# Adding up gathered expert rows on the tensor engine: a diagonal of slot weights as stationary operand instead of a scaled row and eight transposing matmuls

## The chip, the cores and the metric

One Trainium2 chip, one of its cores. The metric is the device time of one execution in microseconds (us), the median over the runs shown. The engines are named as in the profile: PE (TensorE; PEld are its weight loads), DVE (VectorE), ACT (ScalarE), POOL (GpSimd) and SP (SyncE, which only issues transfers here).

## The reference

One decoder layer over 1024 positions of width 1024, all in float32: an S5 group and an attention group side by side, an output projection, and then a PEER layer, which is where the change lies. For each position the PEER layer takes 8 heads, finds for each the 16 best of 128 x 128 experts, and adds up 128 expert rows:

```python
idx = e1 * PEER_N_KEYS + e2
g = jax.nn.softmax(top_s, axis=-1).astype(hc.dtype)
u = expert_down[idx]
a = jax.nn.gelu(jnp.einsum('thkd,td->thk', u, hc))
return jnp.einsum('thk,thkd->td', g * a, expert_up[idx])
...
return x + gate_f * peer_ffn(h2, w_query, sub_keys, expert_down, expert_up)
```

The host lays `expert_down` and `expert_up` beside each other, so that one gathered row of 2048 values holds both.

## The kernel before, in words

Three short phases come first (modulation and input projection, the S5 recurrence, the latent projections of the attention). The last phase, `phase_ef`, takes some 85% of the time. It is one loop over 1024 **slots**, written out in the same order on every engine. The 1024 positions are 8 tiles of 128 (one position per partition); slot n belongs to tile n // 128 and is one (head, rank) pair of it. For slot n:

- POOL (L1192) gathers 128 rows of 8 KB, one per partition, with an indirect DMA into `pair[n % 9]`: columns 0 to 1023 are the down row, 1024 to 2047 the up row. Before it may, it waits until `up_used` has reached n - 8, that is until PE has finished with the buffer's last content.
- DVE (L1693, `dot`) multiplies the down row by `h2` and sums it into one value per position, `a`.
- ACT (`gelu`) takes the GELU of that value (L1488), multiplies it by the gate `g` into `w` (L1490), and scales the 1024 columns of the up row by `w` in place (L1492), which counts `scaled` up.
- PE (`add_up`, L1357) waits for `scaled` and runs eight transposing matmuls of 128 x 128 against the identity. They add into one of two PSUM accumulators, `acc_a` and `acc_b`, so that a tile's sum over its 128 slots stands there transposed (model column on the partition).

After a tile's last slot, DVE's `finish` (L1700) multiplies the sum by the gate column `mod` into `gated`, PE's `turn_back` (L1366) transposes it back in eight steps into the PSUM tile `turns`, and DVE's `close` (L1706) adds the residual `x2s` and leaves the result in `h2`, from where SP stores it.

Into this loop other work is set at fixed slots by tables of the kernel (`AT_SCORES`, `AT_TURN`, `AT_VALUES`, `AT_EXP`, `PROJECT`, `ASKED`, `SCORED`, `WEIGHED`): the attention of tiles 2 to 7 at slots 8 to 188; the output projection of those tiles at slots 191 to 246 (24 pieces of 4 matmuls of 512 columns); the query projections for later slots (`queries`, L1332, 16 matmuls of 128 columns, about one group for every 16 slots) with their scores (L1342); and the exponentials of the gates (`softened`, L1483, for every second group of 16 slots), for which ACT loads another table and, for the next GELU, loads that one again. Every engine works its list strictly in order.

Of the kernel before, what the change touches and what calls it, by code (L numbers as in the profile page):

```python
# [16 lines left out]
ALU = mybir.AluOpType  # L17
ACT = mybir.ActivationFunctionType
AX = mybir.AxisListType

P = 128
D = 1024
KD = D // P
SEQ = 1024
NT = SEQ // P
# [12 lines left out]
PH, PK, TOPK = 8, 128, 16  # L38
# [14 lines left out]
SHIFT_M, SCALE_M, GATE_M, SHIFT_F, SCALE_F, GATE_F = 0, 8, 16, 24, 32, 40  # L53
# [31 lines left out]
def place(nc, name, shape, kb, dt=FP32):  # L85
    return nc.alloc_sbuf_tensor_at(name, shape, dt, offset=BIG + int(kb * KB))
# [6 lines left out]
def bcast(ap, axis, shape):  # L93
    return ap.unsqueeze(axis).to_broadcast(shape)
# [844 lines left out]
def phase_ef(nc, A, S):  # L939
# [22 lines left out]
    qt_pair = place(nc, "qt_pair", [P, 2, 2, P], 149)  # L962
    pieces = place(nc, "pieces", [P, 2, KD, PK], 152)
    x2s = place(nc, "x2s", [P, D], 152)
    gated = place(nc, "gated", [P, KD, P], 156)
    h2t = place(nc, "h2t", [P, 2, KD, P], 160)
    staged = place(nc, "staged", [P, 10, 2, PK], 168)
    cand = place(nc, "cand", [P, TOPK, TOPK], 178)
# [2 lines left out]
    sk = place(nc, "sk", [P, 2, PK], 180)  # L971
    qt_one = place(nc, "qt_one", [P, 2, P], 182)
    wq = [place(nc, f"wq{n}", [P, 4, KD, PK], kb) for n, kb in enumerate((136, 32, 48, 64))]
    row_cols = (S.mod[:, GATE_M:GATE_M + KD], S.a_f[:], S.mod[:, SHIFT_F:SHIFT_F + KD])
    yst_kept = nc.dram_tensor("yst_kept", (P, NT - FIRST, KS, P), FP32, kind="Internal").ap()
    rows_kept = nc.dram_tensor("rows_kept", (P, 3, D), FP32, kind="Internal").ap()

# [55 lines left out]

    ACC = (0, 0, 0, 1, 0, 1, 0, 1)
    END = {P * (i + 1) + (1 if i < 2 else 8): i for i in range(NT - 1)}

    with ExitStack() as ctx:
        small = lambda *a: ctx.enter_context(nc.sbuf_tensor(*a))
# [32 lines left out]
        piece_in = [sem(f"g_piece{n}") for n in range(2)]  # L1071
        wq_in = [sem(f"g_wq{n}") for n in range(4)]
        pair_in = [sem(f"g_pair{n}") for n in range(R)]
        dotted, up_used, w_ready, ga_ready, scaled = sem("g_dot"), sem("g_upused"), sem("g_w"), sem("g_ga"), sem("g_sc")
        less_ready, exp_ready, idx_ready, g_ready = sem("g_less"), sem("g_exp"), sem("g_idx"), sem("g_gate")
        t_done, q_done, q_out, s_done, s_out, s_read = (sem(f"g_{n}") for n in ("t", "q", "qo", "s", "so", "sr"))
        acc_read, fin_ready, stored, spilled, x2s_in, back_done = (sem(f"g_{n}") for n in ("acc", "fin", "st", "spill", "x2s", "back"))
        block = ctx.enter_context(nc.Block())
        tile = lambda i: slice(i * P, (i + 1) * P)
        half = lambda buf, m: buf[:, (m % 2) * 512:(m % 2) * 512 + 512] if items[m][0] < 4 else buf[:]  # L1080
# [114 lines left out]
        @block.tensor  # L1195
        def _(pe):
            t = nc.tensor
            evicted = {"act": 0, "dve": 0, "closed": 0}
            waited = dict(evicted)
            turned_out, yat_out, pts_out = {}, {}, {}  # L1200

            def turns_free():
                for name, s in (("act", tt_out), ("dve", b_read), ("closed", fin_ready)):
                    if evicted[name] > waited[name]:
                        pe.wait_ge(s, evicted[name])
                        waited[name] = evicted[name]
# [138 lines left out]
            def add_up(n):  # L1345
                i = n // P
                if n == 0:
                    pe.wait_ge(a_out, FIRST)
                elif n % P == 0 and i < 3:
                    pe.wait_ge(acc_read, i)  # L1350
                elif n == 3 * P:
                    pe.wait_ge(a_out, NT)
                elif n % P == 0:
                    pe.wait_ge(acc_read, i - 1)
                pe.wait_ge(scaled, n + 1)
                for k in range(KD):
                    last = t.matmul(accs[ACC[i]][:, k * P:(k + 1) * P], pair[n % R][:, D + k * P:D + (k + 1) * P], S.ident[:],  # L1357
                                    is_transpose=True, start=n % P == 0 and k % 4 == 0, stop=n % P == P - 1,
                                    skip_group_check=True)
                last.then_inc(up_used, 1)  # L1360

            def turn_back(i):
                pe.wait_ge(acc_read, i + 1)
                turns_free()
                for k in range(KD):
                    last = t.transpose(tt[:, k * P:(k + 1) * P], gated[:, k, :], S.ident[:])  # L1366
                last.then_inc(back_done, 1)
                evicted["closed"] = i + 1

            row(0)  # L1370
            at_scores(0)
# [25 lines left out]
            for n in range(SLOTS):  # L1397
                if n in AT_SCORES:
                    at_scores(AT_SCORES[n])
                if n in AT_BACK:  # L1400
                    at_back(AT_BACK[n])
                if n in AT_TURN:
                    at_turn(AT_TURN[n])
                if n in AT_VALUES:
                    at_values(AT_VALUES[n])
                for part_ in range(2):
                    if n - part_ in PROJECT:
                        project_ssm(PROJECT[n - part_], (part_,))
                    if n - 4 - part_ in PROJECT:
                        project_att(PROJECT[n - 4 - part_], (part_,))  # L1410
                if n in TURNED:
                    turn(TURNED[n])
                if n in ASKED:
                    queries(ASKED[n], (0,) if WIDE(ASKED[n]) else (0, 1))
                if n - 2 in ASKED and WIDE(ASKED[n - 2]):
                    queries(ASKED[n - 2], (1,))
                if n in SCORED:
                    scores(SCORED[n])
                if n - 2 in END:
                    turn_back(END[n - 2])  # L1420
                add_up(n)
            turn_back(NT - 1)

        @block.scalar
        def _(act):
# [59 lines left out]
            def gelu(n):  # L1485
                k = (n // TOPK) % (2 * PH)
                act.wait_ge(dotted, n + 1)
                s_.activation(ga[:, n % NA:n % NA + 1], a[:, n % NA:n % NA + 1], ACT.Gelu_apprx_tanh).then_inc(ga_ready, 1)  # L1488
                act.wait_ge(ga_ready, n + 1)
                s_.activation(w[:, n % NA:n % NA + 1], ga[:, n % NA:n % NA + 1], ACT.Copy, scale=g[:, k, n % TOPK:n % TOPK + 1]).then_inc(w_ready, 1)  # L1490
                act.wait_ge(w_ready, n + 1)
                s_.activation(pair[n % R][:, D:], pair[n % R][:, D:], ACT.Copy, scale=w[:, n % NA:n % NA + 1]).then_inc(scaled, 1)  # L1492

            for m in range(EARLY):
                at_exp(m)
# [46 lines left out]
        def _(dve):  # L1542
# [139 lines left out]
            def weigh(batch):  # L1682
                first, end = BATCHES[batch]
                at_, to = first % (2 * PH), (end - 1) % (2 * PH) + 1
                dve.wait_ge(exp_ready, batch + 1)
                own.step(v.tensor_reduce(gs[:, at_:to], g[:, at_:to, :], AX.X, ALU.add))
                own.step(v.reciprocal(gs[:, at_:to], gs[:, at_:to]))
                v.tensor_tensor(g[:, at_:to, :], g[:, at_:to, :], bcast(gs[:, at_:to], 2, [P, end - first, TOPK]), ALU.mult).then_inc(g_ready, 1)

            def dot(n):  # L1690
# [2 lines left out]
                v.scalar_tensor_tensor(down, down, 1.0, h2[:, n // P, :], ALU.mult, ALU.mult,  # L1693
                                       accum_out=a[:, n % NA:n % NA + 1]).then_inc(dotted, 1)

            def finish(i):
                dve.wait_ge(up_used, P * (i + 1))
                if i == 0:
                    dve.wait_ge(q_done, PH + 1)
                v.tensor_tensor(gated[:], accs[ACC[i]][:].rearrange("p (k n) -> p k n", n=P),  # L1700
                                bcast(S.mod[:, GATE_F:GATE_F + KD], 2, [P, KD, P]), ALU.mult).then_inc(acc_read, 1)

            def close(i):
                dve.wait_ge(back_done, i + 1)
                dve.wait_ge(x2s_in, 16 * (i + 1))
                v.tensor_tensor(h2[:, i, :], tt[:], x2s[:], ALU.add).then_inc(fin_ready, 1)  # L1706

            at_top(0)
            for m in range(EARLY):
# [24 lines left out]
            for n in range(SLOTS):  # L1734
                dot(n)
                if n in FOUND:
                    find_part(*FOUND[n])
                if n in AT_TOP:
                    at_top(AT_TOP[n])
                if n - 1 in AT_BACK:  # L1740
                    at_back(AT_BACK[n - 1])
                if n in AT_TURNED:
                    at_turned(AT_TURNED[n])
                if n in AT_NORMAL:
                    at_normal(AT_NORMAL[n])
                if n - 8 in PROJECT:
                    combine(PROJECT[n - 8])
                if n - 9 in PROJECT:
                    add_x(PROJECT[n - 9])
                if n - 13 in PROJECT:  # L1750
                    make_h2(PROJECT[n - 13])
                if n - 14 in PROJECT:
                    shift_h2(PROJECT[n - 14])
                if n in WEIGHED:
                    own.wait()
                    weigh_less(WEIGHED[n])
                if n - 2 in WEIGHED:
                    weigh(WEIGHED[n - 2])
                if n in END:
                    finish(END[n])  # L1760
                if n - 3 in END:
                    close(END[n - 3])
# [49 lines left out]
```

## Time and profile before

| | |
|---|---|
| runs | 3248.62, 3248.66, 3250.68 us; median 3248.66 |
| span of the profiled execution | 3247.0 us |
| PE busy | 2362.8 us (73%) |
| DVE busy | 2206.0 us (68%) |
| ACT busy | 2035.2 us (63%) |
| POOL busy | 1321.2 us (41%) |
| gathered by the indirect DMA | 1077.61 MB, its packets 81% of 16 engines' span |
| L1357 (the additions) on PE | 8192 matmuls, 878.7 and 592.6 us in the two accumulators |
| L1492 (the scaling) on ACT | 1024 times 1149 ns |

The profiled execution's own time is its span, 3247.0 us, 1.7 us under the median of the runs. "Busy" is the union of an engine's instructions. The granted clock is the share of TensorE's 2.4 GHz that it was given; at any moment it is 1.0 (2.4 GHz) or 0.5 (1.2 GHz), and the numbers between are means over a stretch. A float32 matmul that multiplies stands in the trace as two MATMUL records and two LDWEIGHTS records; a transposing one as one of each.

### The profile page before, as it was taken

What the parts mean: (1) busy time and instruction counts of PE and PEld (TensorE: products, weight loads), DVE (VectorE), ACT (ScalarE), POOL (GpSimd) and SP (SyncE); (2) the same over time, 40 slices, a digit from 0 to 9 for tenths busy, and PEclk for the clock granted to TensorE, in tenths of its full rate; (3) what the DMA queues carried; (4) which work ended last, traced back from release to release, by engine and by line L of the source; (5) the groups of instructions that cost most, each with busy time, mean ns of one, the idle gap of its engine ahead of it and who ended that gap; (6) DMA issues with size and microseconds to landing.
All of it is one profiled execution on the core that took longest, in us unless ns stands there. A gap on an engine that the chain in (4) does not pass through costs nothing.

```text
span 3247.0 us, 38518 instructions
## 1 busy us (share of the span) xinstructions
PE 2362.8 (73%) x13186; PEld 1943.1 (60%) x13186; DVE 2206.0 (68%) x5266; ACT 2035.2 (63%) x3762; POOL 1321.2 (41%) x1190
## 2 busy tenths in 40 slices
PE   5977787777778797676676677766767667776766
PEld 4654456666666565565665566665666566665655
DVE  6881547767778576677666666666666666666654
ACT  3313416767777566676666766676667766766665
POOL 1140313323434344444445454444444444544543
PEclk9988998988878798777767776777677777767766
DMA  6600039988888999999999999999999999999997
GB/s 250 189 14 4 34 146 419 386 320 322 345 335 346 418 419 420 420 421 421 421 422 420 418 421 419 419 411 420 421 419 413 419 417 418 415 417 419 418 420 326
DMA packets 175461, 1162.57 MB, mean 358 GB/s; under 512 B 22720, under 2 KB 23632, under 8 KB 43808
## 3 DMA queue, kind: packets, MB, share of 16 engines
q0 software_dynamic: 148352, 1077.61, 81.0%
q1 hardware_dynamic: 25680, 78.30, 6.5%
q10 hardware_dynamic: 1232, 4.20, 0.3%
q8 instruction: 104, 1.70, 0.2%
q14 instruction: 93, 0.76, 0.1%
HBM read 1147.32 MB, written 11.53 MB: 357 GB/s over the span
## 4 chain that ended last, share of the span: by engine, by line
DMA 33%; DVE 23%; PE 16%; ACT 11%; issue 4%; POOL 1%; POOLq 0%; DVEq 0%; SPq 0%
DMA pair<-in_experts_dram,idx_g 32%; DVE pair L1693 11%; PE acc_a L1357 5%; ACT pair L1492 5%; PE pef L1332 3%; PE acc_b L1357 2%; ACT L1488 2%; PE acc_b L1237 1%; ACT w L1490 1%; PE pef L1256 1%; ACT pex L1433 1%; DVE top_i L1621 1%; DVE staged L1622 1%; ACT ga L1488 1%; DVE top_i L1624 1%
## 5 line engine op out<-in xcount | busy, mean ns | idle before, releaser
L1192 POOL DMA_INDIRECT pair<-in_experts_dram,idx_g x1024 | 1215.8, 1187 | 1484.1 <-PE acc_a L1357 865.1
L1693 DVE SCALAR_TENSOR_TENSOR pair<-pair,h 128x1024 f32<-128x1024 f32 x1024 | 1247.3, 1221 | 666.2 <-DMA pair<-in_experts_dram,idx_g 664.7
L1357 PE MATMUL acc_a<-ident,pair 128*128 128x128 f32 x5120 | 878.7, 333 | 443.2 <-ACT pair L1492 435.4
L1492 ACT ACTIVATE pair<-pair,w 128x1024 f32<-128x1024 f32 x1024 | 1176.2, 1149 | 33.3
L1357 PEld LDWEIGHTS acc_a<-ident,pair 128*128 128x128 f32 x5120 | 738.1, 173 | 576.3 <-ACT pair L1492 546.0
L1357 PE MATMUL acc_b<-ident,pair 128*128 128x128 f32 x3072 | 592.6, 361 | 292.9 <-ACT pair L1492 292.4
L1357 PEld LDWEIGHTS acc_b<-ident,pair 128*128 128x128 f32 x3072 | 488.6, 187 | 391.4 <-ACT pair L1492 386.7
L1488 ACT ACTIVATE ga<-a 128x1 f32<-128x1 f32 x1024 | 204.1, 199 | 687.3 <-DVE pair L1693 682.5
L1490 ACT ACTIVATE w<-ga,g 128x1 f32<-128x1 f32 x1024 | 301.6, 295 | 33.2
L1332 PE MATMUL pef<-h2t,wq 128*128 128x128 f32 x1536 | 196.6, 291 | 1.6 <-DMA wq<-in_w_query_t_dram 1.6
L1332 PEld LDWEIGHTS pef<-h2t,wq 128*128 128x128 f32 x1536 | 195.0, 209 | 2.8 <-issue 2.8
L1563 DVE TENSOR_SCALAR_CACHE_REDUCE pex<-acc_b 128x128 f32<-128x128 f32 (+7 forms) x64 | 48.3, 754 | 83.1 <-PE turns L1245 43.8
L1237 PE MATMUL acc_b<-kt,qt 96*128 96x512 f32 (+3 forms) x192 | 95.2, 582 | 0.3 <-DVE pex L1563 0.2
L1256 PEld LDWEIGHTS pef<-v,pts 128*128 128x128 f32 x576 | 78.8, 212 | 10.3 <-issue 4.8
L1693 DVE DVE_READ_ACCUMULATOR pair<-pair,h 128x1 f32 x1024 | 84.5, 82 | 0.0
L1256 PE MATMUL pef<-v,pts 128*128 128x64 f32 x576 | 80.3, 290 | 3.6 <-DVE pts L1574 2.1
L401 DVE SCALAR_TENSOR_TENSOR wada<-wada,silu_c 128x1024 f32<-128x1024 f32 x48 | 57.5, 1221 | 18.3 <-DMA wada<-in_w_ada_t_dram 17.7
L1332 PE MATMUL pef<-h2t,pieces 128*128 128x256 f32 (+1 forms) x288 | 64.0, 383 | 3.5 <-ACT h2t L1459 2.2
L1488 ACT ACT_TABLE_LOAD x50 | 64.2, 1283 | 0.9
L1574 DVE COPY pts<-turns 128x128 f32<-128x128 f32 (+7 forms) x64 | 48.2, 753 | 21.5 <-PE pef L1256 14.0
L1467 ACT ACTIVATE qt_one<-pef 128x256 f32<-128x256 f32 x50 | 19.1, 382 | 69.0 <-PE pef L1332 68.9
L1332 PEld LDWEIGHTS pef<-h2t,pieces 128*128 128x128 f32 x288 | 54.6, 214 | 12.1 <-issue 3.4
(341 smaller groups left out, 2365.6 us busy)
## 6 DMA issues: line engine op xcount, KB each, us to landing
wada<-in_w_ada_t_dram SPq DMA_DIRECT2D x48, 512.0 KB, 5.8
pair<-in_experts_dram,idx_g POOLq DMA_INDIRECT x1024, 16.2
pieces<-in_w_query_t_dram SPq DMA_DIRECT2D x16, 512.0 KB, 8.2
wq<-in_w_query_t_dram SPq DMA_DIRECT2D x4, 2048.0 KB, 35.9
ht<-in_x_t_dram ACTq DMA_DIRECT2D x4, 1024.0 KB, 15.1
wout_a<-in_w_out_dram SPq DMA_DIRECT2D x1, 4096.0 KB, 13.1
x2s<-out_dram SPq DMA_DIRECT2D x8, 512.0 KB, 12.3
out_dram<-h SPq DMA_DIRECT2D x8, 512.0 KB, 8.9
```

The lines of the kernel that those rows point to most:

```text
L401: v.scalar_tensor_tensor(wb, wb, 1.0, silu_c[:], ALU.mult, ALU.mult, accum_out=macc[:, b:b + 1]).then_inc(w_used, 1)
L1192: p.indirect_dma_start(pair[n % R], None, A["experts"], bass.IndirectOffsetOnAxis(ap=idx[:, t % (2 * PH), k:k + 1], axis=0)).then_inc(pair ...
L1237: last = t.matmul(sc[:, b:end], S.qt[:, i, h, :], S.kt[:, h, b:end], start=not diagonal, stop=True, skip_group_check=True)
L1256: last = t.matmul(ob[:, h * DV:(h + 1) * DV], half(pts, m)[:, b * P:(b + 1) * P], S.v[:, b, h * DV:(h + 1) * DV], start=b == 0, stop=b == i)
L1332: last = t.matmul(view(qs[:, n * wide:(n + 1) * wide]), weight[:, k, :], h2t[:, :, k, :] if WIDE(q) else h2t[:, min(to, 1), k, :], start=k ...
L1357: last = t.matmul(accs[ACC[i]][:, k * P:(k + 1) * P], pair[n % R][:, D + k * P:D + (k + 1) * P], S.ident[:], is_transpose=True, start=n % ...
L1488: s_.activation(ga[:, n % NA:n % NA + 1], a[:, n % NA:n % NA + 1], ACT.Gelu_apprx_tanh).then_inc(ga_ready, 1)
L1490: s_.activation(w[:, n % NA:n % NA + 1], ga[:, n % NA:n % NA + 1], ACT.Copy, scale=g[:, k, n % TOPK:n % TOPK + 1]).then_inc(w_ready, 1)
L1492: s_.activation(pair[n % R][:, D:], pair[n % R][:, D:], ACT.Copy, scale=w[:, n % NA:n % NA + 1]).then_inc(scaled, 1)
L1563: v.tensor_scalar(probs(m)[:, 0:n], half(pb, m)[:, 0:n], -SCALE, None, ALU.mult, ALU.min, accum_out=top[:, m:m + 1]).then_inc(top_ready, 1)
L1574: v.tensor_copy(half(pts, m)[:, 0:n], half(tt, m)[:, 0:n]).then_inc(tt_out, 1)
L1693: v.scalar_tensor_tensor(down, down, 1.0, h2[:, n // P, :], ALU.mult, ALU.mult, accum_out=a[:, n % NA:n % NA + 1]).then_inc(dotted, 1)
```

## The change

ACT no longer scales the up row. It writes a 128 x 128 diagonal instead, the identity with each row scaled by that position's `w`, into the single tile `diag`. PE takes `diag` as stationary operand and passes the up row, as it was gathered, through it as moving operand: two float32 matmuls of 512 columns. The sum then stands in PSUM with the position on the partition. The eight transposes back at a tile's end go away; for them a row of the gate, `grow`, is made once at slot 126 (`gate_row` on PE, `gate_row_out` on DVE), and `finish` and `close` work on 1024 columns as before.

```diff
-    gated = place(nc, "gated", [P, KD, P], 156)
+    grow = place(nc, "grow", [P, D], 156)
+    diag = place(nc, "diag", [P, P], 199)
...
-                pe.wait_ge(scaled, n + 1)
-                for k in range(KD):
-                    last = t.matmul(accs[ACC[i]][:, k * P:(k + 1) * P], pair[n % R][:, D + k * P:D + (k + 1) * P], S.ident[:],
-                                    is_transpose=True, start=n % P == 0 and k % 4 == 0, stop=n % P == P - 1,
-                                    skip_group_check=True)
+                pe.wait_ge(diag_ready, n + 1)
+                for m in range(2):
+                    last = t.matmul(accs[ACC[i]][:, m * 512:(m + 1) * 512], diag[:], pair[n % R][:, D + m * 512:D + (m + 1) * 512],
+                                    start=n % P == 0, stop=n % P == P - 1, skip_group_check=True)
                 last.then_inc(up_used, 1)
 
-            def turn_back(i):
-                pe.wait_ge(acc_read, i + 1)
+            def gate_row():
                 turns_free()
                 for k in range(KD):
-                    last = t.transpose(tt[:, k * P:(k + 1) * P], gated[:, k, :], S.ident[:])
-                last.then_inc(back_done, 1)
-                evicted["closed"] = i + 1
+                    last = t.transpose(tt[:, k * P:(k + 1) * P], row_cols[3][:, k:k + 1].to_broadcast([P, P]), S.ident[:])
+                last.then_inc(rows_done, 1)
+                evicted["gate_row"] = 4
...
-                s_.activation(pair[n % R][:, D:], pair[n % R][:, D:], ACT.Copy, scale=w[:, n % NA:n % NA + 1]).then_inc(scaled, 1)
+                if n >= 1:
+                    act.wait_ge(up_used, n)
+                s_.activation(diag[:], S.ident[:], ACT.Copy, scale=w[:, n % NA:n % NA + 1]).then_inc(diag_ready, 1)
...
+            def gate_row_out():
+                dve.wait_ge(rows_done, 4)
+                dve.wait_ge(q_done, PH + 1)
+                v.tensor_copy(grow[:], tt[:]).then_inc(rows_out, 1)
...
-                v.tensor_tensor(gated[:], accs[ACC[i]][:].rearrange("p (k n) -> p k n", n=P),
-                                bcast(S.mod[:, GATE_F:GATE_F + KD], 2, [P, KD, P]), ALU.mult).then_inc(acc_read, 1)
+                v.tensor_tensor(h2[:, i, :], accs[ACC[i]][:], grow[:], ALU.mult).then_inc(acc_read, 1)
...
-                v.tensor_tensor(h2[:, i, :], tt[:], x2s[:], ALU.add).then_inc(fin_ready, 1)
+                v.tensor_tensor(h2[:, i, :], h2[:, i, :], x2s[:], ALU.add).then_inc(fin_ready, 1)
```

PE's list before, at a query group in the later part of the loop (`g_sc` is the semaphore `scaled`; L1357 is `add_up`, L1332 `queries`):

```order
L1357 MATMUL acc_b<-ident,pair8_2704 128x128 [waits g_sc]
L1357 MATMUL acc_b<-ident,pair8_2704 128x128 x7
L1332 MATMUL pef1<-h2t_2716,wq2_2725 128x128 [waits g_wq2,g_so,e_tto]
L1332 MATMUL pef1<-h2t_2716,wq2_2725 128x128 x7
L1332 MATMUL pef1<-h2t_2716,wq2_2725 128x128 [waits g_wq2]
L1332 MATMUL pef1<-h2t_2716,wq2_2725 128x128 x7
L1357 MATMUL acc_b<-ident,pair0_2696 128x128 [waits g_sc]
L1357 MATMUL acc_b<-ident,pair0_2696 128x128 x7
```

The same place of PE's list in the changed kernel (`g_dg` is `diag_ready`; L1359 is `add_up`, L1334 `queries`):

```order
L1359 MATMUL acc_b<-pair8_2704,diag_2716 128x512
L1334 MATMUL pef1<-h2t_2717,wq2_2726 128x128 [waits g_wq2,g_so,e_tto]
L1334 MATMUL pef1<-h2t_2717,wq2_2726 128x128 x7
L1334 MATMUL pef1<-h2t_2717,wq2_2726 128x128 [waits g_wq2]
L1334 MATMUL pef1<-h2t_2717,wq2_2726 128x128 x7
L1359 MATMUL acc_b<-pair0_2696,diag_2716 128x512 [waits g_dg]
L1359 MATMUL acc_b<-pair0_2696,diag_2716 128x512
L1359 MATMUL acc_b<-pair1_2697,diag_2716 128x512 [waits g_dg]
```

No work is moved here: the queries stand between the same slots, and each slot's eight matmuls have become two.

ACT's list before, around the exponentials of the gates (L1488 is the GELU, L1490 `w`, L1492 the scaling, L1483 the exponential):

```order
L1490 ACTIVATE w<-ga,g 128x1 [waits g_ga]
L1492 ACTIVATE pair3_2699<-pair3_2699,w 128x1024 [waits g_w]
L1483 ACT_TABLE_LOAD
L1483 ACTIVATE g<-g 128x32 [waits g_less]
L1488 ACT_TABLE_LOAD
L1488 ACTIVATE ga<-a 128x1 [waits g_dot]
L1490 ACTIVATE w<-ga,g 128x1 [waits g_ga]
L1492 ACTIVATE pair4_2700<-pair4_2700,w 128x1024 [waits g_w]
```

The same place of ACT's list in the changed kernel (L1487 the GELU, L1489 `w`, L1493 the diagonal; `g_upused` is `up_used`):

```order
L1489 ACTIVATE w<-ga,g 128x1 [waits g_ga]
L1493 ACTIVATE diag_2716<-ident,w 128x128 [waits g_upused,g_w]
L1482 ACT_TABLE_LOAD
L1482 ACTIVATE g<-g 128x32 [waits g_less]
L1487 ACT_TABLE_LOAD
L1487 ACTIVATE ga<-a 128x1 [waits g_dot]
L1489 ACTIVATE w<-ga,g 128x1 [waits g_ga]
L1493 ACTIVATE diag_2716<-ident,w 128x128 [waits g_upused,g_w]
```

The order is the same; what ACT writes is one tile for all slots instead of nine buffers in turn, and each write now waits for PE as well.

## Rows read from the trace of the kernel before

**Rows 1.** The page: span, clock and DMA share in 40 slices, issues (median to landing).

```profile
span 3247.0 us, 38518 instructions
...
PEclk9988998988878798777767776777677777767766
DMA  6600039988888999999999999999999999999997
...
pair<-in_experts_dram,idx_g POOLq DMA_INDIRECT x1024, 16.2
```

**Rows 2.** L1492 alone, once per slot, in three stretches: duration min/median/max, first and last start.

```profile
L1492 ACT ACTIVATE pair<-pair,w x192: 1147/1148/1160, 493.1 to 1089.6; 128x1024 f32<-128x1024 f32 x192
...
L1492 ACT ACTIVATE pair<-pair,w x759: 1147/1148/1155, 1312.8 to 3237.2; 128x1024 f32<-128x1024 f32 x190
```

**Rows 3.** Windows: length, busy PE, PEld, DVE, ACT, POOL; clock, DMA share, GB/s.

```profile
493.00:1093.00 600.00, 459.10 (x2848) 394.69 (x2848) 444.36 (x1113) 427.24 (x764) 225.58 (x203) 0.84 0.91 357
1093.00:1313.00 220.00, 180.32 (x908) 124.75 (x908) 145.82 (x265) 135.86 (x249) 92.70 (x86) 0.89 1.01 419
1313.00:3240.00 1927.00, 1349.89 (x7772) 1160.28 (x7772) 1324.41 (x3217) 1332.55 (x2439) 904.58 (x751) 0.72 1.01 416
```

**Rows 4.** Timeline near the end: start, duration, engine, what [idle before, releaser].

```profile
3226.07 1.97 PE L1357 MATMUL acc_b<-ident,pair 128*128 128x128 f32 x8 [0.79 <-ACT pair L1492]
...
3226.80 0.20 ACT L1488 ACTIVATE ga<-a 128x1 f32<-128x1 f32 x1 [0.78 <-DVE pair L1693]
3227.04 0.30 ACT L1490 ACTIVATE w<-ga,g 128x1 f32<-128x1 f32 x1
...
3229.27 0.20 ACT L1488 ACTIVATE ga<-a 128x1 f32<-128x1 f32 x1 [0.75 <-DVE pair L1693]
```

**Rows 5.** Timeline, PE alone: two trains of float32 matmuls of 512 columns.

```profile
129.54 14.13 PE L378 MATMUL rb<-win_s,ht 128*128 128x512 f32 x32
...
427.14 7.09 PE L1281 MATMUL acc_a<-wout_a,yst 128*128 128x512 f32 x16
```

**Rows 6.** Timeline at 2904: ACT ends, PE loads, multiplies, ACT reads.

```profile
2904.95 0.53 PEld L1342 LDWEIGHTS pef<-skt,qt_one 128*128 128x128 f32 x4
2905.06 0.61 PE L1342 MATMUL pef<-skt,qt_one 128*128 128x128 f32 x4
2905.70 0.38 ACT L1476 ACTIVATE staged<-pef 128x256 f32<-128x256 f32 x1
```

**Rows 7.** Lines of ACT: busy, mean ns of one, idle before.

```profile
L1492 ACT ACTIVATE pair<-pair,w 128x1024 f32<-128x1024 f32 x1024 | 1176.2, 1149 | 33.3
L1490 ACT ACTIVATE w<-ga,g 128x1 f32<-128x1 f32 x1024 | 301.6, 295 | 33.2
...
L273 ACT ACTIVATE ct_lat<-pa,cols 128x128 f32<-128x128 f32 x24 | 7.1, 375 | 1.0 <-PE pa L348 1.0
```

**Rows 8.** Timeline, PE: one query group, at two places.

```profile
2004.09 4.35 PE L1332 MATMUL pef<-h2t,wq 128*128 128x128 f32 x32
...
2654.25 3.74 PE L1332 MATMUL pef<-h2t,wq 128*128 128x128 f32 x32
```

**Rows 9.** Timeline, ACT alone: the exponentials of the gates between two slots.

```profile
1547.86 1.28 ACT L1483 ACT_TABLE_LOAD   x1
1549.15 0.23 ACT L1483 ACTIVATE g<-g 128x32 f32<-128x32 f32 x1
```

**Rows 10.** Timeline, ACT: the attention's exponentials between two slots.

```profile
805.36 1.28 ACT L1433 ACT_TABLE_LOAD   x1
...
810.14 0.29 ACT L1490 ACTIVATE w<-ga,g 128x1 f32<-128x1 f32 x1
```

**Rows 11.** Waits between 500 and 1050 us: total, times, longest.

```profile
DVE pex L1563 <- PE turns L1245: 43.8, 10, 9.9
```

**Rows 12.** One window of 50 us with the output projection in it, columns as in rows 3.

```profile
1150.00:1200.00 50.00, 45.70 (x230) 30.63 (x231) 36.86 (x75) 31.63 (x59) 22.75 (x22) 0.97 1.01 421
```

**Rows 13.** Timeline, the last transposes back.

```profile
3240.83 1.85 PE L1366 MATMUL turns<-ident,gated 128*128 128x128 f32 x8 [1.32 <-DVE gated L1700]
```

More of the change, by code:

```diff
@@ L973, in phase_ef @@
     wq = [place(nc, f"wq{n}", [P, 4, KD, PK], kb) for n, kb in enumerate((136, 32, 48, 64))]
-    row_cols = (S.mod[:, GATE_M:GATE_M + KD], S.a_f[:], S.mod[:, SHIFT_F:SHIFT_F + KD])
+    row_cols = (S.mod[:, GATE_M:GATE_M + KD], S.a_f[:], S.mod[:, SHIFT_F:SHIFT_F + KD], S.mod[:, GATE_F:GATE_F + KD])
     yst_kept = nc.dram_tensor("yst_kept", (P, NT - FIRST, KS, P), FP32, kind="Internal").ap()
@@ L1035, in phase_ef @@
     END = {P * (i + 1) + (1 if i < 2 else 8): i for i in range(NT - 1)}
+    GATE_ROW_AT = P - 2
     with ExitStack() as ctx:
@@ L1073, in phase_ef @@
         pair_in = [sem(f"g_pair{n}") for n in range(R)]
-        dotted, up_used, w_ready, ga_ready, scaled = sem("g_dot"), sem("g_upused"), sem("g_w"), sem("g_ga"), sem("g_sc")
+        dotted, up_used, w_ready, ga_ready, diag_ready = sem("g_dot"), sem("g_upused"), sem("g_w"), sem("g_ga"), sem("g_dg")
         less_ready, exp_ready, idx_ready, g_ready = sem("g_less"), sem("g_exp"), sem("g_idx"), sem("g_gate")
         t_done, q_done, q_out, s_done, s_out, s_read = (sem(f"g_{n}") for n in ("t", "q", "qo", "s", "so", "sr"))
-        acc_read, fin_ready, stored, spilled, x2s_in, back_done = (sem(f"g_{n}") for n in ("acc", "fin", "st", "spill", "x2s", "back"))
+        acc_read, fin_ready, stored, spilled, x2s_in = (sem(f"g_{n}") for n in ("acc", "fin", "st", "spill", "x2s"))
         block = ctx.enter_context(nc.Block())
@@ L1197, in _ @@
             t = nc.tensor
-            evicted = {"act": 0, "dve": 0, "closed": 0}
+            evicted = {"act": 0, "dve": 0, "gate_row": 0}
             waited = dict(evicted)
@@ L1202, in turns_free @@
             def turns_free():
-                for name, s in (("act", tt_out), ("dve", b_read), ("closed", fin_ready)):
+                for name, s in (("act", tt_out), ("dve", b_read), ("gate_row", rows_out)):
                     if evicted[name] > waited[name]:
@@ L1418, in _ @@
                     scores(SCORED[n])
-                if n - 2 in END:
-                    turn_back(END[n - 2])
+                if n == GATE_ROW_AT:
+                    gate_row()
                 add_up(n)
-            turn_back(NT - 1)
         @block.scalar
@@ L1698, in finish @@
                 if i == 0:
-                    dve.wait_ge(q_done, PH + 1)
-                v.tensor_tensor(gated[:], accs[ACC[i]][:].rearrange("p (k n) -> p k n", n=P),
-                                bcast(S.mod[:, GATE_F:GATE_F + KD], 2, [P, KD, P]), ALU.mult).then_inc(acc_read, 1)
+                    dve.wait_ge(rows_out, 4)
+                v.tensor_tensor(h2[:, i, :], accs[ACC[i]][:], grow[:], ALU.mult).then_inc(acc_read, 1)
             def close(i):
-                dve.wait_ge(back_done, i + 1)
+                dve.wait_ge(acc_read, i + 1)
                 dve.wait_ge(x2s_in, 16 * (i + 1))
-                v.tensor_tensor(h2[:, i, :], tt[:], x2s[:], ALU.add).then_inc(fin_ready, 1)
+                v.tensor_tensor(h2[:, i, :], h2[:, i, :], x2s[:], ALU.add).then_inc(fin_ready, 1)
             at_top(0)
@@ L1758, in _ @@
                     weigh(WEIGHED[n - 2])
+                if n == GATE_ROW_AT + 1:
+                    gate_row_out()
                 if n in END:
```

## The prediction, made blind

> **What bounds the kernel now.** I read the page first. Its slices [rows 1] show the DMA engines at 0.9 or more of their time from about slice 13 to the end, while TensorE's clock is granted at 0.6 to 0.8. Then I took the start of L1492, which runs once per slot, as a clock of the loop [rows 2]. Slots 0 to 191, which carry the attention (stage A), take 493 to 1093 us, that is 600 us or 3.13 us a slot. Slots 265 to 1023 (stage C) take 1924 us, 2.54 us a slot. The 73 slots between, with the output projection (stage B), take 220 us. The three windows [rows 3] show what sets each. In B and C the DMA share is 1.01 at 416 to 419 GB/s: the gather itself is the limit. In A it is 0.91 and no engine is full (PE 459 of 600, DVE 444, ACT 427): there the engines wait for each other. The timeline of three late slots [rows 4] shows the undisturbed beat: the GELUs start 2.47 us apart, and ACT waited 0.75 us for DVE, which waited for the transfer. PE sits idle within each slot although each set of eight transposes ran at 1.2 GHz (1.97 us).
>
> **What a slot costs after the change.** PE: the trains of 512-column float32 matmuls [rows 5] give the time between records: (14.13 - 0.59) / 31 = 0.437 us and (7.09 - 0.59) / 15 = 0.433 us, where 0.59 us is one record from start to end. These trains are two records for one matmul, so a slot's two matmuls are four records: 1.73 us of streaming, and 3 x 0.433 + 0.592 = 1.89 us from the first record's start to the last one's end, at 2.4 GHz. Eight transposes, 1.97 us at 1.2 GHz [rows 4], take about half of that at this clock, so PE's own work per slot nearly doubles, although the instructions fall from eight to two.
>
> ACT: the scaling of 1149 ns goes. In its place a 128 x 128 copy with a scale column: the nearest row is L273, the same shape and kind, 375 ns [rows 7]. That row reads PSUM; from 128x1 (295 ns) and 128x1024 (1149 ns) on the same operands one gets 295 + 127 x 0.835 = 401 ns. I take 0.38 us, with 0.295 and 0.40 as the ends. ACT gains 0.77 us a slot.
>
> The wait: there is one `diag`. ACT may write slot n's only when PE has ended slot n-1's, and PE may start slot n only when it is written. Before, nine buffers kept the two apart. So in slots with no other PE work the two run strictly in turn: diagonal 0.38, ACT's end to the first weight load 0.05, weight load ahead of the first matmul 0.11 (2904.95 to 2905.06), matmuls 1.89, PE's end to ACT's start 0.03 (2905.67 to 2905.70) [rows 6]. Sum **2.46 us**. The GELU and `w` (0.20 and 0.30 us [rows 4]) fit on ACT under the 1.9 us of PE. So the turn costs PE a gap of 2.46 - 1.73 = 0.73 us whenever nothing else fills it. 2.46 us is just what the gather takes too. Every piece of other work that PE or ACT has comes on top, where before it was hidden in the gather's time. That is the core of the forecast: a loop bound by transfers with PE to spare becomes one bound by the turn between PE and ACT. Behind the waiting diagonal on ACT stand the copies of queries and scores and the exponentials; behind the waiting matmuls on PE stands everything of the next slot; and POOL waits for `up_used`, but nine buffers are 22 us of turns, and a gather lands 16.2 us after its issue even with the queues full [rows 1].
>
> Clock: in the window with the projection trains [rows 12] PE was busy 45.7 of 50 us and the granted clock was 0.97. In stage C it was 0.72 with PE busy 0.70 [rows 3], much of that at 1.2 GHz, where records take longer. With four 512-column records in every slot PE is busy for 1.9 of 2.46 us plus the queries, 80% or more at 2.4 GHz. I take 2.4 GHz throughout.
>
> **Stage C.** 759 x 2.46 = 1867 us. 45 query groups: 32 records in 3.74 us at 2.4 GHz, about 3.6 us of streaming [rows 8]; the diagonal is written meanwhile, so each adds 3.6 - 0.73 = 2.87 us, 129 us in all. (With 4.35 us it would be 34 us more.) 23 exponentials of the gates: from a diagonal's end, table 1.28, exp 0.23, table 1.28 again [rows 9], GELU 0.20, `w` 0.30, diagonal 0.38 and 0.26 of hand-overs make 3.93 us to the next stream, where a plain slot has 0.16 + 1.73 + 0.73 = 2.62: 1.3 us each, 30 us. Scores (0.45 us of PE) hide in the gap. Sum 2026 us against 1924: **+102**.
>
> **Stage B.** 73 x 2.46 = 180; 24 pieces of projection of 8 records, 3.47 us each, add 2.74: 66; three query groups 9. Sum 255 against 220: **+35**.
>
> **Stage A.** 192 x 2.46 = 472. Other PE work at 2.4 GHz: scores of 48 blocks, 33,792 columns or 57 us at the train's rate; values, 528 records of 0.11 us (the query group's rate), 58 us; 264 transposes at 0.12, 31; twelve half groups of wide queries, 16 records of 256 columns at 0.217 us, 42; the rest 20. That is 208 us in 116 of the 192 slots; each hides up to 0.73 us of the gap, leaving 126 us. 24 times ACT does the attention's exponentials between two slots: 805.36 to 810.43 [rows 10] is 5.1 us before the diagonal, 4.7 on the mean of all sizes, so 5.2 to the next stream, 2.6 over a plain slot: 62. Sum 660. The waits of DVE's running minimum for PE's transposes that are there now (44 us between 500 and 1050 [rows 11]) come from the minimum that may not overwrite a buffer before PE has turned it; with PE's steps longer they reach through to the next dot product. I bound what they add by 0 and 44 and take 25. So 685 against 600: **+85**. ACT's relief is spent in the turn.
>
> **End.** Eight transposes and their hand-over after the last slot go, 1.9 us [rows 13]. The gate row costs 2 us at slot 126 once, half of it hidden.
>
> Total: 85 + 35 + 102 - 2 = +220 on the profiled execution's 3247.0 us: 3467 us. The runs' median stood 1.7 us above that execution, so **3469 us**, 6.8% more.
>
> **Rivals.** (1) *The clock stays low.* If it sat at 1.2 GHz, a record streams 0.853 us and the turn is 0.57 + 3 x 0.853 + 1.02 = 4.15 us: 1024 x 1.69 more, over 5100 us. Against it, the 0.97 above. Half the time low would give about 4300 us, but PE would then be busy nearly all the time. Chance 3%. (2) *The hand-over is hidden.* If ACT's end, weight load and PE's end together cost 0.25 us a slot less than in rows 6 and 7, stage C comes to about 2.42 us a slot on average, below the gather's 2.5; C and B stay and only A's coupling counts, some +0 to +60. That needs the matmuls to release ACT before their last results are in, which no row shows. Chance 3% that it ends within 0.2%. (3) *Faster, through stage A.* ACT is 0.77 us a slot lighter. If A's present slack comes from ACT alone, and PE's part of the turn stays under the gather's beat, A falls towards the gather's 192 x 2.5 = 480 us with C unchanged: down to 3127 us, half of it 3187. It decides where four records take under 1.4 us in place of 1.89. The trains say 0.433 us a record and leave no room. Chance 4%.
>
> The Trainium skill speaks for this third case (page "TensorE: Matmul & The Clock Gate", section "Back-to-back issue gap"): in a stream of weight loads and matmuls it gives a sustained roofline of about 131 ns per matmul at N = 512. As an estimate from that page, four records would stream in 0.52 us, the turn would be 1.56 us, the gather would stay the limit and the time would be near 3187 us. This case's trace does not agree: 0.433 us a record over trains of 16 and 32.
>
> The same page (section "Part 4: PE-mode transpose") says that transposing matmuls do not count as activity for the full clock. If so, multiplying ones should only help the clock here, which is against rival 1. The trace before has both kinds mixed in every stage and does not show that by itself.
>
> **Chances and range.** The forecast case has 90%. Within it: the diagonal between 0.295 and 0.40 us (-87 to +20), the exposed weight load 0 to 0.11 (-80 to 0 where the gaps show), query groups at 4.35 (+34), DVE's waits (-25 to +19). Not all at once: 3400 to 3560 us. The rivals outside it hold 10%. By 0.2%, 6.5 us, which is what runs of this kernel can tell from no change: faster 4%, same 3%, slower 93%.
>
> **What the trace will show.** Right: the diagonal at 0.38 us starting 0.03 us after PE's last record; four records of 0.59 us, 0.43 apart; 2.46 us between diagonals in plain slots; granted clock 0.95 or more in stage C; DMA share there near 0.94; stage starts at 685, 255 and 2026 us; ACT idle behind PE. Wrong: gaps between diagonals of 2.5 us with DMA share at 1.0 (rival 2), records of 1.0 us (rival 1), stage A under 600 us (rival 3). An error in the turn counts 1024 times, so 0.05 us there moves the result by 51 us.

## The result and the profile after

The changed kernel takes 3557.69 us (median of 4 runs, 3554.46 to 3564.9) against 3248.64 us for the kernel before on the same chip: a ratio of 1.096, with a 95% interval of 1.094 to 1.098 (estimated over all runs; the two medians by themselves divide to 1.095). It is slower by 309 us, where 220 us were forecast. The direction and the mechanism held; the rise was 1.4 times the forecast one, and that is what the sections below are about.

The page of the changed kernel (span, granted clock and DMA share in 40 slices), which answers to [rows 1]:

```profile
span 3552.6 us, 31231 instructions
...
PEclk8988999999999999999999999999999999999999
DMA  6500269887778978999999999999999999999997
...
PE 67%; ACT 15%; issue 3%; DVE 2%; DMA 1%; ACTq 0%; POOL 0%; DVEq 0%; POOLq 0%
```

The last of these lines is the chain of work that ended last, by engine. Before, DMA had 33% of it and PE 16%; now PE has 67%, ACT 15% and DMA 1%. The clock sits at 0.9 or more from slice 5 on.

Its longest waits (who waited for whom: us in total, times, longest):

```profile
ACT diag L1493 <- PE acc_a L1359: 1229.8, 597, 8.3
POOL pair L1194 <- PE acc_a L1359: 1149.3, 583, 7.9
PEld acc_a L1359 <- ACT diag L1493: 694.2, 494, 4.8
ACT diag L1493 <- PE acc_b L1359: 683.9, 372, 4.5
```

ACT waits for PE before 597 + 372 = 969 of the 1024 diagonals, and PE's weight loads wait for ACT nearly as often. That is the turn that the prediction spoke of. The timeline of PE, of its weight loads and of ACT at a place with no other work shows each part of it:

```profile
2499.67 1.98 PE L1359 MATMUL acc_b<-pair,diag 128*128 128x512 f32 x4 [0.55 <-ACT diag L1493]
...
2502.21 0.30 PEld L1359 LDWEIGHTS acc_b<-pair,diag 128*128 128x128 f32 x2 [1.38 <-ACT diag L1493]
2502.21 1.98 PE L1359 MATMUL acc_b<-pair,diag 128*128 128x512 f32 x4 [0.55 <-ACT diag L1493]
2504.75 0.70 PE L1359 MATMUL acc_b<-pair,diag 128*128 128x512 f32 x1 [0.55 <-ACT diag L1493]
...
2501.76 0.40 ACT L1493 ACTIVATE diag<-ident,w 128x128 f32<-128x128 f32 x1 [1.72 <-PE acc_b L1359]
2502.06 0.19 ACT L1487 ACTIVATE ga<-a 128x1 f32<-128x1 f32 x1
2502.28 0.29 ACT L1489 ACTIVATE w<-ga,g 128x1 f32<-128x1 f32 x1
...
2504.29 0.40 ACT L1493 ACTIVATE diag<-ident,w 128x128 f32<-128x128 f32 x1 [1.72 <-PE acc_b L1359]
```

From diagonal to diagonal it is 2.53 us: diagonal 0.40, hand-over to PE 0.05 (2502.16 to 2502.21), records 1.98 (to 2504.19), hand-over to ACT 0.10 (to 2504.29). (The profile models the ends of matmuls, so the split between the last two is less sure than their sum.) GELU and `w` lie under PE's records and cost nothing, as forecast. The last PE line is cut off where its view ends and so shows a turn's first record alone: 0.70 us.

The windows of the three stages, cut where the diagonals of slots 0, 192 and 265 start (columns as in [rows 3]):

```profile
494.00:1197.00 703.00, 600.82 (x2096) 327.27 (x2097) 447.85 (x1121) 276.99 (x765) 215.07 (x203) 0.94 0.84 312
1197.00:1458.00 261.00, 230.50 (x593) 99.56 (x591) 142.15 (x258) 75.81 (x247) 93.19 (x86) 1.00 0.85 336
1458.00:3545.00 2087.00, 1681.12 (x4692) 711.12 (x4692) 1307.75 (x3219) 698.85 (x2440) 899.34 (x751) 1.00 0.98 383
```

Stage A took 703 us (600 before), B 261 (220), C 2087 (1924). The gather fell from 416 to 383 GB/s in stage C: it is no longer the limit. The end after the last slot:

```profile
3545.08 1.98 PE L1359 MATMUL acc_b<-pair,diag 128*128 128x512 f32 x4 [0.55 <-ACT diag L1493]
...
3547.10 1.22 DVE L1706 TENSOR_TENSOR h<-acc_b,grow 128x1024 f32<-128x1024 f32 x1 [13.53 <-PE acc_b L1359]
3548.36 1.23 DVE L1711 TENSOR_TENSOR h<-h,x2s 128x1024 f32<-128x1024 f32 x1
```

The two DVE steps now follow each other directly; the transposes of [rows 13] between them are gone.

### The profile page after: what moved, and what is told of

Read it like the earlier page. It is cut to its first block, busy times and chain, and to the rows that moved or that the text cites. A ratio compares the mean times of both kernels' runs of the same rounds, so it can differ in the third digit from the quotient of the medians.

```text
span 3552.6 us, 31231 instructions
## 1 busy us (share of the span) xinstructions
PE 2887.0 (81%) x9034; PEld 1401.6 (39%) x9034; DVE 2189.4 (62%) x5267; ACT 1190.8 (34%) x3762; POOL 1305.3 (37%) x1190
## 4 chain that ended last, share of the span: by engine, by line
PE 67%; ACT 15%; issue 3%; DVE 2%; DMA 1%; ACTq 0%; POOL 0%; DVEq 0%; POOLq 0%
PE acc_a L1359 32%; PE acc_b L1359 21%; ACT diag L1493 10%; PE pef L1334 6%; PE acc_b L1239 2%; ACT L1487 2%; PE pef L1258 2%; PE acc_b L1283 1%; PE turns L1299 1%; ACT pex L1432 1%; ACT L1482 1%; PE turns L1247 1%; ACT L1432 1%; DMA pair<-in_experts_dram,idx_g 1%; DVE pair L1694 1%
## 5 line engine op out<-in xcount | busy, mean ns | idle before, releaser
L1359 PE MATMUL acc_a<-pair,diag 128*128 128x512 f32 x2560 | 1285.4, 625 | 320.9 <-ACT diag L1493 316.1
L1694 DVE SCALAR_TENSOR_TENSOR pair<-pair,h 128x1024 f32<-128x1024 f32 x1024 | 1231.1, 1218 | 406.6 <-DMA pair<-in_experts_dram,idx_g 405.9
L1493 ACT ACTIVATE diag<-ident,w 128x128 f32<-128x128 f32 x1024 | 411.1, 401 | 1915.5 <-PE acc_a L1359 1229.8
L1359 PE MATMUL acc_b<-pair,diag 128*128 128x512 f32 x1536 | 762.1, 619 | 207.7 <-ACT diag L1493 205.5
L1359 PEld LDWEIGHTS acc_a<-pair,diag 128*128 128x128 f32 x2560 | 445.5, 192 | 1030.4 <-ACT diag L1493 694.2
L1359 PEld LDWEIGHTS acc_b<-pair,diag 128*128 128x128 f32 x1536 | 260.9, 189 | 680.3 <-ACT diag L1493 491.7
L1489 ACT ACTIVATE w<-ga,g 128x1 f32<-128x1 f32 x1024 | 301.6, 295 | 33.1
L1621 DVE MAX8 top_v<-staged 128x8 f32<-128x128 f32 x128 | 37.3, 291 | 279.7 <-ACT staged L1475 279.7
L1487 ACT ACTIVATE ga<-a 128x1 f32<-128x1 f32 x1024 | 192.9, 188 | 40.7 <-DVE pair L1694 40.1
L1334 PEld LDWEIGHTS pef<-h2t,wq 128*128 128x128 f32 x1536 | 179.1, 192 | 23.0 <-issue 23.0
L1334 PE MATMUL pef<-h2t,wq 128*128 128x128 f32 x1536 | 179.2, 275 | 0.0
L1239 PE MATMUL acc_b<-kt,qt 96*128 96x512 f32 (+3 forms) x192 | 81.7, 507 | 0.0
L1334 PE MATMUL pef<-h2t,pieces 128*128 128x256 f32 (+1 forms) x288 | 61.8, 374 | 3.6 <-ACT h2t L1458 2.2
```

The source lines that it names most:

```text
L1239: last = t.matmul(sc[:, b:end], S.qt[:, i, h, :], S.kt[:, h, b:end], start=not diagonal, stop=True, skip_group_check=True)
L1334: last = t.matmul(view(qs[:, n * wide:(n + 1) * wide]), weight[:, k, :], h2t[:, :, k, :] if WIDE(q) else h2t[:, min(to, 1), k, :], start=k ...
L1359: last = t.matmul(accs[ACC[i]][:, m * 512:(m + 1) * 512], diag[:], pair[n % R][:, D + m * 512:D + (m + 1) * 512], start=n % P == 0, stop=n ...
L1493: s_.activation(diag[:], S.ident[:], ACT.Copy, scale=w[:, n % NA:n % NA + 1]).then_inc(diag_ready, 1)
```

## The experiments

Theory T: the turn between ACT and PE over the one diagonal costs the time. Theory P: PE's four passes a slot are too much work by themselves. Eight further kernels bear on them. Stage lengths in this table are taken between the starts of `w` in slots 0, 192, 265 and 1023; for the changed kernel this puts 8 us of stage A's 703 into stage B.

| kernel | median us | ratio to before (95%) | A | B | C |
|---|---|---|---|---|---|
| before | 3248.64 | | 600 | 220 | 1924 |
| changed | 3557.69 | 1.096 (1.094 to 1.098) | 695 | 269 | 2085 |
| two diagonals | 3291.57 | 1.015 (1.012 to 1.017) | 617 | 244 | 1926 |
| three diagonals | 3277.85 | 1.009 (1.008 to 1.011) | 603 | 247 | 1923 |
| one diagonal, half the columns | 3283.61 | 1.011 (1.010 to 1.013) | 615 | 227 | 1934 |
| old form with the turn | 3932.04 | 1.211 (1.209 to 1.213) | 698 | 256 | 2470 |
| longer turn | 3840.10 | 1.183 (1.181 to 1.185) | 733 | 279 | 2320 |
| longer turn, two diagonals | 3309.57 | 1.019 (1.018 to 1.021) | 629 | 248 | 1923 |
| three diagonals, half the columns | 3210.35 | 0.989 (0.987 to 0.990) | 561 | 221 | 1922 |
| old form, half the scaling | 3226.58 | 0.993 (0.992 to 0.995) | 579 | 222 | 1923 |

The kernel before had a median of 3246.4 us beside the eight experiments, and their ratios are to those runs.

### Two diagonals

```diff
-    diag = place(nc, "diag", [P, P], 199)
+    ND = 2
+    diag = [place(nc, "diag", [P, P], 199)[:]] + [S.rope[:, n].rearrange("p i f -> p (i f)") for n in range(ND - 1)]
...
-                    last = t.matmul(accs[ACC[i]][:, m * 512:(m + 1) * 512], diag[:], pair[n % R][:, D + m * 512:D + (m + 1) * 512],
+                    last = t.matmul(accs[ACC[i]][:, m * 512:(m + 1) * 512], diag[n % ND], pair[n % R][:, D + m * 512:D + (m + 1) * 512],
...
-                if n >= 1:
-                    act.wait_ge(up_used, n)
-                s_.activation(diag[:], S.ident[:], ACT.Copy, scale=w[:, n % NA:n % NA + 1]).then_inc(diag_ready, 1)
+                if n >= ND:
+                    act.wait_ge(up_used, n + 1 - ND)
+                s_.activation(diag[n % ND], S.ident[:], ACT.Copy, scale=w[:, n % NA:n % NA + 1]).then_inc(diag_ready, 1)
```

> The changed kernel with two diagonal tiles used in turn (the second lies in the memory of the rope table, which is dead by then), so that ACT may write slot n's while PE still reads slot n-1's. Theory T (the turn between ACT and PE is what costs: 2.54 us a slot of which PE streams 1.72): PE's records now follow each other without the gap of 0.8 us, stage C goes back to the gather's limit, 1924 us as before, stage B to 220-235, stage A to 590-620 (the exponentials still stop ACT for 5 us); total 3250 us, 3220 to 3290. Theory P (the four passes themselves are too much work for PE, the hand-over is a minor part): the time stays above 3450 us and PE is busy over 90% in stage C. Rival of my own on the size: if only the 0.55 us of ACT's part is hidden and not the 0.1 us at PE's end, stage C is still the gather's.

Measured: 3291.57 us, just above the expected range's 3290, and 266 us under the changed kernel. Stage C is back at 1926 us. Its windows:

```profile
494.00:1110.00 616.00, 563.55 (x2084) 324.15 (x2084) 444.52 (x1113) 284.98 (x762) 221.59 (x203) 0.96 0.91 346
1110.00:1355.00 245.00, 228.31 (x604) 106.86 (x604) 145.46 (x263) 78.69 (x248) 99.42 (x86) 0.97 0.95 377
1355.00:3280.00 1925.00, 1612.83 (x4690) 725.35 (x4691) 1323.18 (x3219) 775.12 (x2438) 990.09 (x751) 0.99 1.01 416
```

PE does the same work as in the changed kernel (4690 records in stage C against 4692), and the gather is again at 416 GB/s and a share of 1.01, as in [rows 3]. Theory P falls for stage C. In stage B PE is busy 228 of 245 us, and stage B came out 9 us above what theory T gave it: there PE's work itself may count, which the run with three diagonals and half the columns tests.

### Three diagonals

As above with `ND = 3`.

> As the run with two diagonals, with three. Theory T: nothing more in stage C and B, where the gather is the limit; in stage A ACT may run one slot further ahead before an exponential stops it, so 0 to 25 us less than with two. Theory P: no difference from two, and both above 3450 us.

Measured: 3277.85 us, 14 us under two diagonals, all of it in stage A (617 to 603), as theory T has it. Still 0.9% slower than before, and not in stage C.

### One diagonal, half the columns

The second matmul of each slot is left out, so half of the PEER sum is missing.

```diff
-                for m in range(2):
+                for m in range(1):
                     last = t.matmul(accs[ACC[i]][:, m * 512:(m + 1) * 512], diag[:], pair[n % R][:, D + m * 512:D + (m + 1) * 512],
```

> The changed kernel (one diagonal) with the second matmul of each slot left out, so that columns 512 to 1023 of the PEER sum are missing. Turn 0.40 + 0.05 + 1.13 + 0.10 = 1.68 us, under the gather's 2.5. Both theories: stage C at 1924-1950 us, B near 220. Stage A 560 to 600: 192 x 1.68 + about 150 + 62 + waits of DVE. Total 3220 us, 3180 to 3270. If it stays over 3300 us, something other than the length of the turn (the gather itself being slower, DVE) makes the changed kernel slow, and both theories are wrong.

Measured: 3283.61 us, 14 us above the expected range. Stage C took 1934 us, as expected, so neither the gather nor DVE holds it up in the changed kernel. Both theories expected that, so this run does not tell them apart: the missing matmul shortens the turn and PE's work alike. Stage A missed: 615 us, where 560 to 600 were expected. The granted clock is lower here (0.83 in stage A, 0.72 in stage C), and PE's timeline shows both lengths of the same pair of records:

```profile
2500.01 1.13 PE L1359 MATMUL acc_b<-pair,diag 128*128 128x512 f32 x2 [1.05 <-ACT diag L1493]
2503.04 2.07 PE L1359 MATMUL acc_b<-pair,diag 128*128 128x512 f32 x2 [1.90 <-ACT diag L1493]
```

The expectation had priced every record at 2.4 GHz. That this is the whole of stage A's miss was not tested by itself; with three diagonals and the same two records a slot, at a clock of 0.86, stage A took 561 us, 54 us less at nearly the same clock, so the low clock without the turn does not give 615 us.

### The old form in the new turn

```diff
                 act.wait_ge(w_ready, n + 1)
+                if n >= 1:
+                    act.wait_ge(up_used, n)
                 s_.activation(pair[n % R][:, D:], pair[n % R][:, D:], ACT.Copy, scale=w[:, n % NA:n % NA + 1]).then_inc(scaled, 1)
```

> The kernel before, with the one wait added: ACT scales slot n's up row only when PE has ended slot n-1's transposes. The old operations in the new turn. Theory T: turn 1.15 + 0.05 + 1.09 + 0.10 = 2.39 us at 2.4 GHz and 3.27 us at 1.2 GHz; with the clock at 1.2 GHz about half the time 2.8 us a slot, plus 45 queries of about 2.4 us: stage C about 2250 us, and the total 3550 to 3750 us, as slow as the changed kernel or slower, though PE does only half the work. Theory P: the wait costs little, since PE has idle time in every slot: under 3330 us.

Measured: 3932.04 us, beyond even theory T's 3750. One wait added to the kernel before costs 686 us, more than twice what the whole change costs, although PE's operations are the old ones. Its timeline, PE alone:

```profile
2607.32 1.09 PE L1357 MATMUL acc_a<-ident,pair 128*128 128x128 f32 x8 [1.30 <-ACT pair L1494]
2609.72 1.09 PE L1357 MATMUL acc_a<-ident,pair 128*128 128x128 f32 x8 [1.30 <-ACT pair L1494]
2612.11 1.97 PE L1357 MATMUL acc_a<-ident,pair 128*128 128x128 f32 x8 [1.30 <-ACT pair L1494]
2615.37 1.97 PE L1357 MATMUL acc_a<-ident,pair 128*128 128x128 f32 x8 [1.30 <-ACT pair L1494]
2618.64 1.97 PE L1357 MATMUL acc_a<-ident,pair 128*128 128x128 f32 x8 [1.30 <-ACT pair L1494]
```

and the window of its stage C (columns as in [rows 3]):

```profile
1448.00:3918.00 2470.00, 1553.62 (x7766) 1309.33 (x7765) 1304.51 (x3214) 1259.56 (x2439) 850.74 (x752) 0.62 0.88 324
```

The two turns are 2.40 us at 2.4 GHz and 3.27 at 1.2 GHz, as worked out (2.39 and 3.27). What the expectation missed is the share of each: it had taken the low clock for about half the time (a mean of 0.75), and the granted clock in stage C was 0.62. At 2.4 GHz the turn of the old operations is 2.40 us, that of the new ones 2.54: the new operations add 0.9 us of PE to a turn and take 0.75 us of ACT out of it, so the two turns are nearly as long, and it is the turn that costs. In the changed kernel the clock was 1.00 in stage C. Why it stayed up there and not here is open: both the amount and the kind of PE's work differ between the two. Multiplying alone does not keep it up, since the run with half the columns, which multiplies too, had 0.72 there.

### A longer turn, with one and with two diagonals

```diff
+                s_.activation(S.rope[:, 1].rearrange("p i f -> p (i f)"), S.ident[:], ACT.Copy, scale=w[:, n % NA:n % NA + 1])
                 s_.activation(diag[:], S.ident[:], ACT.Copy, scale=w[:, n % NA:n % NA + 1]).then_inc(diag_ready, 1)
```

> The changed kernel (one diagonal) with a second 128x128 copy on ACT, of the same form, into memory that nobody reads, between the wait for PE and the diagonal. ACT's copies start 0.30 us apart when back to back, so the turn grows by 0.30 us where nothing else fills the gap: about 850 slots of 1024 (in 172 slots PE's other work covers it). Theory T: 850 x 0.30 = 255 us more than the changed kernel, 3810 us (3770 to 3860), plain slots at 2.84 us. If the turn were not the limit, since ACT is busy only 34% of the time: no change, 3555 us.

> The same extra copy in the kernel with two diagonals. Theory T: the copy lies beside PE's records, stage C stays at 1926 us; stage A has ACT's 0.30 us in the slots around the exponentials, 5 to 20 us more. Total 3290 to 3315 us against 3292 for two diagonals. If ACT's load itself counted, 250 us more.

Measured: 3840.10 us with one diagonal, 282 us more than the changed kernel, where 255 were expected; 3309.57 us with two, 18 us more. ACT's timeline of the first:

```profile
2500.09 0.40 ACT L1493 ACTIVATE rope<-ident,w 128x128 f32<-128x128 f32 x1 [1.45 <-PE acc_a L1359]
2500.39 0.39 ACT L1494 ACTIVATE diag<-ident,w 128x128 f32<-128x128 f32 x1
...
2502.91 0.40 ACT L1493 ACTIVATE rope<-ident,w 128x128 f32<-128x128 f32 x1 [1.72 <-PE acc_a L1359]
```

The plain slot grew from 2.54 to 2.82 us, which over the changed kernel's some 800 plain slots is about 225 us; the rest of the 282 lies in the other slots. The same copy costs 282 us when it lies in the turn, and 18 us when it does not. In stage C with two diagonals it costs nothing (1923 us). ACT's load is not the question; its place in the turn is. It also shows how a small error in the turn's length is multiplied, which is what happened to the prediction.

### Three diagonals and half the columns

Both edits together; half of the PEER sum is missing.

> Three diagonals and the second matmul of each slot left out (columns 512 to 1023 of the PEER sum are missing): PE has 0.86 us a slot instead of 1.72 and no turn. If what is left over the kernel before (0.9% with three diagonals) is PE's doubled streaming in stages A and B, stage B falls from 247 back to 220 us, where the gather is the limit, and stage A from 603 to 540-580; stage C stays at 1924. Total 3180 to 3240 us. If stage A is set by the order of the attention's work on all engines and not by PE's load, A stays at 600 and the total is 3250.

Measured: 3210.35 us. Stage B fell from 247 to 221 us and stage A from 603 to 561. The windows of stages A and B:

```profile
492.00:1053.00 561.00, 449.26 (x1702) 269.41 (x1702) 444.34 (x1114) 288.31 (x763) 237.23 (x203) 0.86 0.95 381
1053.00:1275.00 222.00, 181.62 (x456) 81.13 (x456) 145.70 (x264) 82.56 (x250) 91.73 (x86) 0.87 1.01 419
```

With half the passes stage B is the gather's again (419 GB/s, as in [rows 3]). So what is left with three diagonals is PE's doubled streaming in the two stages where PE has other work: the second matmul costs 42 us in stage A and 26 in stage B, of which ACT's relief gives back 39 (561 against the 600 of the kernel before). Theory P is right there, for the 0.9% (31 us) by which three diagonals stay behind the kernel before.

### The old form with half the scaling

ACT scales only columns 0 to 511 of the up row; the others enter the sum unscaled.

```diff
-                s_.activation(pair[n % R][:, D:], pair[n % R][:, D:], ACT.Copy, scale=w[:, n % NA:n % NA + 1]).then_inc(scaled, 1)
+                s_.activation(pair[n % R][:, D:D + 512], pair[n % R][:, D:D + 512], ACT.Copy, scale=w[:, n % NA:n % NA + 1]).then_inc(scaled, 1)
```

> The kernel before with ACT scaling only 512 of the 1024 up columns (the other 512 enter the sum unscaled), so that ACT has 0.43 us a slot less and PE the same. It prices ACT's relief alone, the gain that the change could have brought. Stages B and C are the gather's: unchanged, 220 and 1924 us. Stage A: if ACT's load is part of its 600 us, 560 to 585; if not, 600. Total 3205 to 3250 us.

Measured: 3226.58 us, 20 us under the kernel before, all in stage A (579 against 600). A relief of ACT by 0.43 us a slot (its copy takes 0.72 us instead of 1.15) is worth 0.1 us a slot in stage A and nothing elsewhere. The change relieves ACT by 0.75 us. What it had within reach was therefore small, between these 20 us and the 39 us that stage A gained with three diagonals and half the columns.

No kernel that does the whole computation was faster than the kernel before. The nearest is the one with three diagonals.

## Why the prediction was right in kind and short in size

**The mechanism held.** The prediction's core, "a loop bound by transfers with PE to spare becomes one bound by the turn between PE and ACT": shown by the waits in both directions, by two diagonals giving stage C back in full, and by the longer turn.

**The step that failed is the sum of the turn, "2.46 us".** It measured 2.536 us in the median plain slot. Its terms, forecast and measured: diagonal 0.38 and 0.401; ACT's end to the weight load 0.05 and 0.05; weight load and records 0.11 + 1.89 = 2.00 and 1.98; PE's end to ACT's start 0.03 and 0.10. The diagonal's 0.02 and PE's hand-over's 0.07, less 0.02 won on the records, are the whole error. That the records came out so close is luck in part: the first weight load had no time of its own (it starts with the first record, at 2502.21), and in its place the first record took 0.70 us and not 0.59, so two errors of about 0.1 us cancelled. The hand-over of 0.03 us was read off [rows 6], where ACT reads what PE has just written in PSUM. Here ACT reads and writes SBUF, and the gap in the records was 0.10 us; it was 0.10 too in the old form with the turn. The trace of the kernel before already held the right row: at its start ACT waits six times until it may overwrite an SBUF tile that PE has read, and each time it starts 0.10 us after PE's recorded end. One of them (PE ends at 22.62):

```profile
22.06 0.57 PE L323 MATMUL pa<-ones_b,sqx 128*128 128x1 f32 x2
...
22.72 1.06 ACT L259 ACTIVATE sqx<-ht 128x1024 f32<-128x1024 f32 x1 [2.36 <-PE pa L323]
```

For the diagonal, L273 [rows 7] reads PSUM as well; the value interpolated from the SBUF rows, 0.401, was in the text as an upper end, and was exact.

**How it grew.** 0.076 us x 1024 slots = 78 us, of the 86 us between the forecast 3467 and the span of 3552.6. By stage, forecast, measured, and what the turn's error explains, counted on every slot: A 685, 703, 15; B 255, 261, 6; C 2026, 2087, 58. What else went into the sums of stages B and C (query groups, projection, exponentials, hidden scores) is confirmed to within about 3 us, as a sum. In stage C the 45 slots with a query group took 5.29 us from diagonal to diagonal, 2.75 over a plain one where 2.87 were forecast, and most of those with an exponential 3.82, 1.28 over a plain one where 1.3 was forecast. In stage A 3 us are left; the 25 us chosen there for DVE's waits were a guess that no run tested by itself.

**The range had no term for it.** The median of 3557.69 us lies only 2 us under the upper end of 3560, and two of the four runs lie above it. The terms that the prediction listed upwards (+20, +34, +19) reach no further than 3469 + 73 = 3542 us. The bounds of the turn's terms (0.295 to 0.40, 0 to 0.11) reached far down and hardly up: no upper end was given for the hand-over that one row had shown. So it is luck, and no term of the sum, that the stated range still holds the median. The prediction itself said that 0.05 us in the turn moves the result by 51 us.

In stage A the prediction's 126 us for PE's other work should read 123 (208 less 116 x 0.73), which changes nothing here.

**The rivals.** Low clock: no, the granted clock was 0.97 over the span and 1.00 in stage C. In two experiments it was lower: with half the columns stage C ran at 0.72, and with the old form in the turn at 0.62. Hidden hand-over: no, PE's end to ACT's start was longer than forecast and not shorter. Faster through stage A: no with one diagonal, and with three stage A is at 603 us against 600, since PE's doubled work takes back what ACT's relief gives. With half the passes the gain is there: 561 us. It is far from the 480 us that this rival had as its lower end.

The rule of the Trainium skill that was weighed (page "TensorE: Matmul & The Clock Gate", section "Back-to-back issue gap", 131 ns per matmul at N = 512) did not hold for these float32 records: from 0.43 us apart in the trains to four in 1.98 us here, of which two make one matmul.

**The end.** From the last diagonal or scaling to the end it is 8.0 us where it was 9.8, so 1.8 us less, where 1.9 were forecast. The step between the two DVE operations went as forecast; the last slot's own work on ACT and PE is 0.1 us longer. **DMA share:** 0.94 was forecast for stage C and 0.98 measured, at 383 GB/s; the share fell less than the rate did, and why was not looked into.

## What to carry to other kernels

Before a per-step operand is made cheaper, count its buffers: nine buffers that the old form happened to use became one, and a loop whose engines ran apart fell into a turn in which every hand-over counts 1024 times. A second copy of the 64 KB tile gave 266 of the 309 us back. And fewer instructions are not less work: two float32 matmuls of 512 columns took 1.98 us where eight transposes of 128 took 1.09, both at 2.4 GHz.

When a turn is priced, take each hand-over from a row with the same engines and the same memories (here it stood in the trace, 0.10 us, six times), and give it an upper end as well as a lower one.

## What the runs showed of the hardware

- PE's recorded end to ACT's start was 0.03 to 0.04 us where ACT read what PE had just written in PSUM, and 0.10 us where ACT overwrote from SBUF a tile in SBUF that PE had just read: in the changed kernel after multiplying records, in the old form with the turn after transposes, and at L259 in the kernel before. Memory and kind of wait changed together in these rows, so which of them makes the difference is open.
- A copy of 128 x 128 with a scale column from SBUF to SBUF took 0.401 us in all 1024 cases (401 to 403 ns), and in the longer turn the second of two such copies started 0.30 us after the first.
- The granted clock of stage C was 1.00 in the changed kernel, with 1.98 us of records in turns of 2.54 us. In the old form with the turn it was 0.62: the lines above show transposes of 1.09 us in turns of 2.40 us at 2.4 GHz, then the fall to 1.2 GHz, and after it 1.97 us of transposes in turns of 3.27 us, turn after turn. There the time was lost in two steps: the turn itself, and the low clock within it. What brought the clock down was not tested by itself.
